# Reading the stationary weight block of the transposed products as every second number of 256

## The chip, the cores and the metric

The kernel runs on one core of one Trainium2 chip. The metric is the device time in microseconds (us) of one execution. Weights lie in HBM in the order in which the host program lays them before the launch; that laying is no part of the time.

## The reference, cut to what matters

Two transformer blocks over 256 tokens of width 2048, in float32. Nearly all of the arithmetic is in eight projections by weight matrices:

```python
z      = rms_norm(x) @ w_in                       # 2048 -> 11264
merged = gate_a * (y_a @ w_branch_a) + gate_b * (y_b @ w_branch_b)
h      = x + merged @ w_out
h      = h + square(relu(rms_norm(h) @ w_up)) @ w_down   # 2048 -> 8192 -> 2048
proj   = rmsnorm(concat(meta, h)) @ w_in_2        # 272 tokens, 2048 -> 6656
h      = h + rmsnorm(concat(ya, yb) @ w_out_2)
```

Between them stand a gated linear recurrence of 8 heads, a banded attention of 16 heads, and in the second block a grouped attention and a differential attention of 8 heads each.

## The kernel before, in words

Every weight matrix is streamed once. It is cut into groups of 512 output columns (`CW`), and a group into 8 chunks of 256 rows (two tiles of 128 rows, 512 columns: 512 KB). A chunk is loaded by SyncE's queue into `raw` (four slots), ScalarE writes its rounded upper part `whi` (L899), VectorE the remainder `wlo = raw - whi` (L1301), both in the type fp32r, and TensorE then makes three products with it: upper by upper, upper by lower, lower by upper. Activations are held in the same two parts (`xhi`/`xlo`, `x2hi`/`x2lo`, `ya_hi`, ...). Semaphores count the chunks: ScalarE waits until TensorE has left the slot, TensorE waits for `wlo_ready`.

There are two ways in which TensorE uses a chunk.

- `chunk_t` (L431 to L448), the transposed one: a block of 128 weight columns is the stationary operand, and the activations (256 tokens, or 272 in the first five groups of `w_in_2`) move past it. The output has the features on the partitions. Per chunk 2 row tiles x 4 blocks x 3 products = 24 matmuls, each of its own weight load. Four blocks of 128 lie side by side in a group, and block b reads columns `slice(b * P, (b + 1) * P)`, 128 adjacent numbers in each partition. All 24 are issued at L446.
- `chunk_n` (L450 to L463), the natural one: 128 tokens of the activations are stationary, and the chunk's 512 columns move. 12 matmuls per chunk, issued at L458.

The transposed way is used for `w_in` except the groups 4, 5, 12 and 13 (18 groups), for `w_branch_a`/`w_branch_b`, `w_up` and all 13 groups of `w_in_2`, the other 8 of which have 256 tokens. The natural one is used for the four other groups of `w_in` and for `w_out`, `w_down` and `w_out_2`.

TensorE runs its instructions in the order of the program: the chunks one after the other, and between them, at places written out by hand, the small matmuls and transposes of the recurrence and of the attentions. `shift_phase` issues three transposes whose output nobody reads. In the recurrence, `level_scores` (L548) has a moving operand whose order depends on the level: 128 numbers of `qp` in runs of 1, 2, 4, ... adjacent numbers (levels 1, 2, 3, ...), while its stationary operand `k_both` is 128 adjacent numbers.

Of the kernel before, what the change touches and what calls it, by code (L numbers as in the profile page):

```python
# [15 lines left out]
P = 128  # L16
# [17 lines left out]
CW = 512  # L34
# [8 lines left out]


C_IN = 0
G_IN = 22
C_BR = C_IN + G_IN * NC
C_OUT = C_BR + 4 * NC
# [13 lines left out]

SETS_BEFORE_2 = (G_IN + 8 + 4 + 32) // 2

# [47 lines left out]
def program(nc, x, w_in, lb_logits, hg_norm_w, rel_bias, w_branch_a, w_branch_b, w_out, norm_mix_w,  # L112
# [3 lines left out]
    with ExitStack() as ctx:  # L116
# [44 lines left out]
        def at(name, kib, shape, dt=F32):  # L161


            with ExitStack() as tmp:
                if kib:
                    tmp.enter_context(nc.sbuf_tensor(name + "_pad", [P, int(kib * 256)], F32))
                return tmp.enter_context(nc.sbuf_tensor(name, shape, dt))
# [21 lines left out]
        pairs = at("pairs", 76, [P, HG, P])  # L189
# [146 lines left out]
        def set_needs():  # L336


            n = [SETS_BEFORE_2 + 3, SETS_BEFORE_2 + 2]
            need = {}  # L340
            for j in range(5, G_IN2):
                s = set_of(j)
                need[j] = n[s]
                n[s] += 1
                if j == 5:
                    n[0] += 1
            return need, n

        need2, sets_before_out2 = set_needs()
        out_free = [G_IN // 2 + 4 + n // 2 + 1 for n in range(4)]  # L350
        down_free = [G_IN // 2 + 8 + 4 * (QUARTERS - 1) + g // 2 + 1 for g in range(4)]

        def wide_hi(kt, n):

            return xw_first[:, kt, 0:n] if kt < WIDE_FIRST else xw_rest[:, kt - WIDE_FIRST, 0:n]
# [10 lines left out]
        def _(sp):  # L366
            def chunk(c0, k, src):

                if not isinstance(c0, int) or c0 + k >= SLOTS:
                    sp.wait_ge(wlo_ready, c0 + k - SLOTS + 1)  # L370
                    sp.sem_inc(sp_turn, 1)
                sp.dma_start(raw[:, k % SLOTS], src).then_inc(raw_in[k % SLOTS], 16)

            def rows(w, k, cols):
                return w[:, CK * k:CK * k + CK, cols]
# [3 lines left out]
            for c in range(4):  # L379
# [6 lines left out]
                else:  # L386
                    chunk(C_IN, c, rows(w_in_t, c, slice(0, CW)))
            for k in range(4, NC):
                chunk(C_IN, k, rows(w_in_t, k, slice(0, CW)))
            with sp.Fori(1, G_IN) as g:  # L390
                for k in range(NC):
                    chunk(C_IN + NC * g, k, rows(w_in_t, k, bass.ds(g * CW, CW)))

# [34 lines left out]
        def _(pe):  # L428
            mm = nc.tensor.matmul

            def chunk_t(c0, k, kt0, xh, xl, outs, n, first, last, shared=True):  # L431

                first_chunk = isinstance(c0, int) and c0 + k == C_IN
                pe.wait_ge(half_lo if first_chunk else wlo_ready, c0 + k + 1)
                for j in range(CK):
                    kt = kt0 + j
                    if first_chunk and j == 1:
                        pe.wait_ge(wlo_ready, 1)  # L440
                    for b in range(4):
                        cols = slice(b * P, (b + 1) * P)
                        x_high = xh[:, kt, 0:n] if xh is not None else wide_hi(kt, n)
                        for i, (w, v) in enumerate(((whi, x_high), (whi, xl[:, kt, 0:n]), (wlo, x_high))):
                            start = first and j == 0 and i == 0 and (b % 2 == 0 or not shared)
                            ins = mm(outs[b], w[:, k % SLOTS, j, cols], v, start=start,  # L446
                                     stop=last and j == CK - 1 and i == 2, skip_group_check=True)
                ins.then_inc(pe_done, 1)  # L448
# [16 lines left out]
            def blocks(s):  # L465
                return [pset(s)[:, b, :] for b in range(4)]
# [14 lines left out]
            def turn_start(c):  # L481

                pe.wait_ge(x_in[c], 16)
                if c >= 2:
                    pe.wait_ge(x_ready, 4 * c - 4)
                for kt in range(4 * c, 4 * c + 4):
                    for t in range(NT):
                        o = (kt % 2) * T + t * P
                        ins = nc.tensor.transpose(ps[:, 4 + (kt % 8) // 2, o:o + P],
                                                  x_nat[:, t, kt * P:(kt + 1) * P], ident[:])  # L490
                    if kt % 2 == 1:
                        ins.then_inc(n_tr, 1)
# [18 lines left out]
            def warm(n):  # L511

                for i in range(n):
                    nc.tensor.transpose(ps[:, 2, 0:P], ident[:], ident[:])
# [100 lines left out]

            for g in range(G_IN):
                c0, s = C_IN + NC * g, g % 2
                if g >= 2:
                    pe.wait_ge(set_free[s], g // 2)
                if g == G_LEVEL:  # L620
                    pe.wait_ge(meta_ready, 1)
                natural = g in (4, 5, 12, 13)
                for k in range(NC):
                    if g == 0:
                        if k == 0:
                            warm(11)
                            turn_start(0)
                            warm(9)
                        if k < 3:
                            turn_start(k + 1)  # L630
                        if k == 3:
                            turn_vectors()
                        if k == 6:
                            row_scale()
                        pe.wait_ge(x_ready, CK * (k + 1))
                    if natural:
                        chunk_n(c0, k, CK * k, uhi, ulo, s, k == 0, k == NC - 1)
                    else:
                        chunk_t(c0, k, CK * k, uhi, ulo, blocks(s), T, k == 0, k == NC - 1)
                    if k == 0 and g == 2:  # L640
                        turn_meta()
                    if k == 1 and G_LEVEL <= g < G_HGOUT:
                        level_scores(g - G_LEVEL)
                    if k == 1 and g == G_HGOUT:
                        hg_output()
                    if k == 7 and g == G_HGOUT:
                        hg_squares()
                    if k == 2 and g == G_HGOUT + 1:
                        pe.wait_ge(hg_sd, 4)
                        shift_phase(4, lambda i: acc[:, i, :])  # L650
                    at = NC * (g - G_ATT) + k
                    for part, late in ((att_values, 5), (att_turn, 4), (att_scores, 0)):
                        if pair_at(at - late) is not None:
                            part(pair_at(at - late))
                    if at == PAIR_STEP * (AH // 2):
                        shift_phase(5, lambda i: prob[:, 0, i * P:(i + 1) * P])
# [1335 lines left out]
    return np.concatenate([np.arange(P), np.arange(T - 1, P - 1, -1)])  # L1992


def shape_constants():

    f32 = np.float32
    identity = np.eye(P, dtype=f32)

    s, t = np.arange(P)[:, None], np.arange(P)[None, :]  # L2000
    masks = np.zeros((P, 8, P), f32)
    masks[:, 0, :] = s == t
    for level in range(1, 8):
        hb = 2 ** (level - 1)
        masks[:, level, :] = (s // (2 * hb) == t // (2 * hb)) & ((s // hb) % 2 != (t // hb) % 2)
    triangles = np.stack([s < t, s > t], axis=1).astype(f32)

    inv_freq = (f32(10000.0) ** (-np.arange(0, DH, 2, dtype=f32) / f32(DH))).astype(f32)
    places = token_order()
    row = np.concatenate([places // 64, np.zeros(META, int)]).astype(f32)  # L2010
    col = np.concatenate([places % 64, np.zeros(META, int)]).astype(f32)
    ang = np.stack([row[:, None] * inv_freq, col[:, None] * inv_freq]).astype(f32)
    half = np.concatenate([ang[0], ang[0], ang[1], ang[1]], axis=1).T
    rope_cos, rope_sin = np.cos(half).astype(f32), np.sin(half).astype(f32)

    turn = np.zeros((P, P), f32)
    for m in range(P):
        if (m // 32) % 2 == 0:
            turn[m + 32, m] = -1.0
        else:  # L2020
            turn[m - 32, m] = 1.0
    qpos = places + META
    kpos = np.concatenate([places + META, np.arange(META)])
    distance = np.abs(qpos[:, None] - kpos[None, :]).astype(f32)
    return {"identity": identity, "level_masks": masks, "rope_cos": rope_cos, "rope_sin": rope_sin,
            "rope_turn": turn, "distance": distance}, {"triangles": triangles}
# [21 lines left out]
```

## Time and profile before

| | us |
|---|---|
| median of 3 runs | 1895.21 |
| lowest and highest run | 1893.33, 1895.46 |
| profiled execution, time | 1893.33 |
| profiled execution, span | 1893.3 |

| engine | busy us | share of the span | instructions |
|---|---|---|---|
| TensorE matmul (PE) | 1879.6 | 99% | 13432 |
| TensorE weight load (PEld) | 1743.7 | 92% | 13432 |
| VectorE (DVE) | 1101.4 | 58% | 1270 |
| ScalarE (ACT) | 889.3 | 47% | 1171 |
| GpSimd (POOL) | 143.6 | 8% | 122 |

How to read it: consecutive matmuls overlap in the records, since each record runs from the start of its operand's reading to a modelled end. The cost of a matmul to the kernel is then the distance from its start to the start of the next one, called its pitch below; durations are only compared with each other. A pitch is read from the start times in a timeline, or from the number of matmuls in a window. A few per cent of the matmul records can be missing, so windows without gaps are used.

### The profile page before, as it was taken

The page shows a single profiled execution, that of the slowest core. Times are in us where ns is not written, and L with a number is a line of the kernel's source. Part 1 is how long each engine was busy: PE and PEld are TensorE (multiplying, and loading weights), DVE is VectorE, ACT ScalarE, POOL GpSimd, SP SyncE. Part 2 cuts the span into 40 slices and gives each one's busy share as a digit, 9 for nine tenths or more (in the row PEclk, how much of TensorE's full clock was granted, in tenths as well). Part 3 has the DMA queues.
Part 4 walks back from the last instruction along what each step waited for, and adds up shares of the span by engine and source line. Part 5 has one row for each costly group of instructions (what it writes and reads, how often), then busy time and mean ns, then how long its engine had stood idle before and what let it go on. Part 6 is the DMA issues. An engine that isn't in the chain of part 4 may idle for free.

```text
span 1893.3 us, 33876 instructions
## 1 busy us (share of the span) xinstructions
PE 1879.6 (99%) x13432; PEld 1743.7 (92%) x13432; DVE 1101.4 (58%) x1270; ACT 889.3 (47%) x1171; POOL 143.6 (8%) x122
## 2 busy tenths in 40 slices
PE   9999999999999999999999999999999999999998
PEld 9989998999999889988998899899889999899986
DVE  6556766667655555545445445445565556767664
ACT  6544444455544445443444344334454355664543
POOL 2001322411001100000010000000010000000000
PEclk9999999999999999999999999999999999999999
DMA  8566565566565656656665665566556655354454
GB/s 270 184 181 177 181 179 178 165 200 180 168 231 191 214 186 179 194 198 192 196 192 193 194 191 194 194 190 190 189 185 181 179 170 150 105 147 144 156 190 143
DMA packets 176434, 346.47 MB, mean 183 GB/s; under 512 B 10976, under 2 KB 11184, under 8 KB 175776
## 3 DMA queue, kind: packets, MB, share of 16 engines
q1 hardware_dynamic: 174176, 337.76, 57.2%
q0 software_dynamic: 2128, 6.82, 1.4%
q8 instruction: 101, 1.65, 0.4%
q14 instruction: 29, 0.24, 0.0%
HBM read 342.44 MB, written 2.10 MB: 182 GB/s over the span
## 4 chain that ended last, share of the span: by engine, by line
PE 97%; DVE 1%; ACT 0%; DMA 0%; issue 0%; SPq 0%; DVEq 0%; ACTq 0%
PE ps L446 58%; PE ps L458 33%; PE ps L548 1%; PE ps L781 1%; DVE wlo L1301 1%; PE ps L771 1%; PE ps L748 1%; PE ps L791 0%; DMA raw<-in_w_in_dram 0%; ACT whi L899 0%; PE ps L476 0%; PE ps L759 0%; PE ps L599 0%; PE ps L591 0%; DVE xlo L1323 0%; PE ps L610 0%
## 5 line engine op out<-in xcount | busy, mean ns | idle before, releaser
L1301 DVE TENSOR_TENSOR wlo<-raw,whi 128x1024 fp32r<-128x1024 f32 x631 | 796.5, 1268 | 698.1 <-ACT whi L899 697.1
L899 ACT ACTIVATE whi<-raw 128x1024 fp32r<-128x1024 f32 x631 | 664.5, 1058 | 886.3 <-PE ps L446 551.5
L446 PE MATMUL ps<-xhi,whi 128*128 128x256 f32 (+1 forms) x1904 | 542.2, 285 | 0.4 <-DVE wlo L1301 0.3
L446 PE MATMUL ps<-xhi,wlo 128*128 128x256 f32 (+1 forms) x1904 | 531.3, 279 | 0.0
L446 PE MATMUL ps<-xlo,whi 128*128 128x256 f32 x1664 | 462.5, 278 | 0.0
L446 PEld LDWEIGHTS ps<-xhi,whi 128*128 128x128 f32 x1904 | 359.1, 189 | 9.3 <-issue 6.7
L446 PEld LDWEIGHTS ps<-xhi,wlo 128*128 128x128 f32 x1904 | 357.8, 188 | 0.0
L446 PEld LDWEIGHTS ps<-xlo,whi 128*128 128x128 f32 x1664 | 313.4, 188 | 1.5 <-issue 0.7
L446 PE MATMUL ps<-x2hi,whi 128*128 128x256 f32 x1024 | 282.8, 276 | 0.0
L446 PE MATMUL ps<-x2hi,wlo 128*128 128x256 f32 x1024 | 282.7, 276 | 0.0
L446 PE MATMUL ps<-x2lo,whi 128*128 128x256 f32 x1024 | 282.7, 276 | 0.0
L446 PEld LDWEIGHTS ps<-x2lo,whi 128*128 128x128 f32 x1024 | 192.2, 188 | 0.2
L446 PEld LDWEIGHTS ps<-x2hi,whi 128*128 128x128 f32 x1024 | 192.2, 188 | 0.2
L446 PEld LDWEIGHTS ps<-x2hi,wlo 128*128 128x128 f32 x1024 | 192.2, 188 | 0.0
L458 PE MATMUL ps<-whi,ya_lo 128*128 128x512 f32 x256 | 100.8, 394 | 0.0
L458 PE MATMUL ps<-whi,yb_lo 128*128 128x512 f32 x256 | 100.8, 394 | 0.0
L458 PE MATMUL ps<-whi,xlo 128*128 128x512 f32 x256 | 100.8, 394 | 0.0
L458 PE MATMUL ps<-wlo,ya_hi 128*128 128x512 f32 x256 | 100.3, 392 | 0.0
L458 PE MATMUL ps<-wlo,yb_hi 128*128 128x512 f32 x256 | 100.2, 392 | 0.0
L458 PE MATMUL ps<-whi,xhi 128*128 128x512 f32 x256 | 100.2, 391 | 0.0
L458 PE MATMUL ps<-wlo,xhi 128*128 128x512 f32 x256 | 100.1, 391 | 0.0
L458 PE MATMUL ps<-whi,ya_hi 128*128 128x512 f32 x256 | 99.7, 390 | 0.0
(373 smaller groups left out, 2370.6 us busy)
## 6 DMA issues: line engine op xcount, KB each, us to landing
raw<-in_w_in_dram SPq DMA_DIRECT2D x279, 512.0 KB, 3.8
raw<-in_w_up_dram SPq DMA_DIRECT2D x128, 512.0 KB, 3.7
raw<-in_w_down_dram SPq DMA_DIRECT2D x128, 512.0 KB, 3.7
raw<-in_w_out_dram SPq DMA_DIRECT2D x64, 512.0 KB, 3.8
raw<-in_w_branch_a_dram SPq DMA_DIRECT2D x16, 512.0 KB, 4.9
raw<-in_w_branch_b_dram SPq DMA_DIRECT2D x16, 512.0 KB, 3.8
x_nat<-in_x_dram SPq DMA_DIRECT2D x4, 512.0 KB, 7.4
rel<-in_rel_turned_dram POOLq DMA_DIRECT2D x8, 256.0 KB, 4.3
```

What stands on the lines that cost most here:

```text
L446: ins = mm(outs[b], w[:, k % SLOTS, j, cols], v, start=start, stop=last and j == CK - 1 and i == 2, skip_group_check=True)
L458: ins = mm(ps[:, 2 * s + t, :], v[:, kt, toks], w[:, k % SLOTS, j, :], start=first and j == 0 and i == 0, stop=last and j == CK - 1 and i ...
L548: ins = mm(misc[:, hd // 4, (hd % 4) * P:(hd % 4 + 1) * P], k_both[:, hd, :], spread(qp[:, hd, 0:1], *both_tiles), start=True, stop=True)
L748: ins = mm(ps[:, 4 + i, 0:TM], qb[f, hd, t * P:(t + 1) * P], kb[f, hd, :], start=True, stop=True)
L771: ins = nc.tensor.transpose(ps[:, 6, i * P:(i + 1) * P], p[:, i * P:(i + 1) * P], ident[:])
L781: ins = mm(ps[:, 7, 0:P], pt2[:, u % 2, i * P:(i + 1) * P], v, start=i == 0, stop=i == 2)
L899: f(whi[:, k % SLOTS], raw[:, k % SLOTS], ACT.Copy).then_inc(whi_ready, 1)
L1301: tt(wlo[:, k % SLOTS], raw[:, k % SLOTS], whi[:, k % SLOTS], ALU.subtract).then_inc(wlo_ready, 1)
```

## The change

`chunk_t` reads block b of a pair as every second number of 256: blocks 0 and 1 are the even and the odd columns of the first 256, blocks 2 and 3 those of the second 256. So that the products stay the same, the host lays the columns of two blocks alternating (`paired`) in `w_branch_a`, `w_branch_b`, `w_up`, `w_in_2`, and in `w_in` except the groups 4, 5, 12 and 13, which are used in the natural way. `chunk_n` is unchanged, as are all loads, waits, tiles and the order of instructions.

```diff
+NATURAL_IN = (4, 5, 12, 13)
...
                     for b in range(4):
-                        cols = slice(b * P, (b + 1) * P)
+                        cols = slice(b // 2 * 2 * P + b % 2, b // 2 * 2 * P + 2 * P, 2)
...
-                natural = g in (4, 5, 12, 13)
+                natural = g in NATURAL_IN
...
+def paired(w, every=True):
+    laid = np.array(w)
+    spans = laid.reshape(*w.shape[:-1], -1, 2, P)
+    pairs = np.swapaxes(spans, -1, -2).reshape(w.shape)
+    if every:
+        return pairs
+    groups = np.arange(w.shape[-1]) // CW
+    return np.where(np.isin(groups, NATURAL_IN), laid, pairs)
...
     laid["x"] = laid["x"][:, places]
+    laid["w_in"] = paired(laid["w_in"], every=False)
+    for name in ("w_branch_a", "w_branch_b", "w_up", "w_in_2"):
+        laid[name] = paired(laid[name])
```

## Rows read from the trace of the kernel before

**Rows 1.** The page: the chain that ended last, by engine and by line

```profile
PE 97%; DVE 1%; ACT 0%; DMA 0%; issue 0%; SPq 0%; DVEq 0%; ACTq 0%
PE ps L446 58%; PE ps L458 33%; PE ps L548 1%; PE ps L781 1%; DVE wlo L1301 1%; PE ps L771 1%; PE ps L748 1%; PE ps L791 0%; DMA raw<-in_w_in_dram 0%; ACT whi L899 0%; PE ps L476 0%; PE ps L759 0%; PE ps L599 0%; PE ps L591 0%; DVE xlo L1323 0%; PE ps L610 0%
```

**Rows 2.** The waits, longest first (us in total, times, longest)

```profile
ACT whi L899 <- PE ps L446: 551.5, 322, 7.0
PE ps L446 <- DVE wlo L1301: 0.3, 1, 0.3
```

**Rows 3.** Windows of L446 alone (stretch: length, PE busy (count), PEld busy (count), clock, DMA)

```profile
30.00:60.00 30.00, 29.80 (x254) 29.70 (x253) 1.00 0.73 229
1080.00:1160.00 80.00, 80.00 (x708) 80.00 (x708) 1.00 0.62 193
```

**Rows 4.** Groups by line and form, TensorE, whole span (count | busy us, mean ns)

```profile
L446 PE MATMUL ps<-xhi,wlo 128*128 128x256 f32 x1664 | 462.5, 278 | 0.0
L446 PE MATMUL ps<-x2hi,wlo 128*128 128x256 f32 x1024 | 282.7, 276 | 0.0
L446 PE MATMUL ps<-xw_lo,whi 128*128 128x272 f32 x320 | 91.7, 287 | 0.0
```

**Rows 5.** Groups by line and form in 30 to 60 us (mean ns behind the comma)

```profile
L446 PE MATMUL ps<-xlo,whi 128*128 128x256 f32 x85 | 23.9, 281 | 0.0
L446 PEld LDWEIGHTS ps<-xlo,whi 128*128 128x128 f32 x84 | 16.1, 192 | 0.0
L446 PEld LDWEIGHTS ps<-xhi,whi 128*128 128x128 f32 x85 | 16.0, 188 | 0.0
```

**Rows 6.** Timeline at 1100 us (start, length, in us)

```profile
1099.99 0.28 PE L446 MATMUL ps<-x2lo,whi 128*128 128x256 f32 x1
1099.99 0.19 PEld L446 LDWEIGHTS ps<-x2hi,wlo 128*128 128x128 f32 x1
1100.10 0.28 PE L446 MATMUL ps<-x2hi,wlo 128*128 128x256 f32 x1
1100.11 0.19 PEld L446 LDWEIGHTS ps<-x2hi,whi 128*128 128x128 f32 x1
1100.22 0.28 PE L446 MATMUL ps<-x2hi,whi 128*128 128x256 f32 x1
```

**Rows 7.** Timeline at 1500 us, TensorE: first and fifth start of 272-column products

```profile
1499.88 0.29 PE L446 MATMUL ps<-xw_lo,whi 128*128 128x272 f32 x1
...
1500.38 0.29 PE L446 MATMUL ps<-xw_rest,wlo 128*128 128x272 f32 x1
```

**Rows 8.** Instructions of L612, L446, L476 (duration ns min/median/max, first and last start us)

```profile
L612 PEld LDWEIGHTS ps<-prob_t,av x32: 137/137/137, 413.2 to 529.3; 128*64 128x64 f32 x32
L446 PEld LDWEIGHTS ps<-x2hi,wlo x1024: 187/188/189, 726.7 to 1339.2; 128*128 128x128 f32 x171
L476 PEld LDWEIGHTS ps<-ident,h x64: 137/141/143, 663.3 to 1436.6; 128*128 128x128 f32 x64
```

**Rows 9.** Instructions of L548 at levels 1, 2 and 3, one window each (same columns)

```profile
L548 PE MATMUL ps<-qp,k_both x16: 324/337/338, 156.6 to 159.1; 128*128 128x128 f32 x16
...
L548 PE MATMUL ps<-qp,k_both x16: 282/283/283, 181.0 to 182.8; 128*128 128x128 f32 x16
...
L548 PE MATMUL ps<-qp,k_both x16: 270/275/275, 204.7 to 206.4; 128*128 128x128 f32 x16
```

**Rows 10.** Windows of L458 alone, in `w_down` (columns as in rows 3)

```profile
840.00:880.00 40.00, 40.00 (x176) 32.84 (x175) 1.00 0.58 190
```

**Rows 11.** Three transposes in the timeline at 1604.7 us, and their mean of one (274 ns)

```profile
1604.74 0.49 PE L771 MATMUL ps<-ident,p 128*128 128x128 f32 x3
...
L771 PE MATMUL ps<-ident,p 128*128 128x128 f32 x96 | 15.9, 274 | 0.8 <-DVE p L1752 0.7
```

**Rows 12.** Groups by line and form in 760 to 800 us

```profile
L1301 DVE TENSOR_TENSOR wlo<-raw,whi 128x1024 fp32r<-128x1024 f32 x15 | 18.3, 1224 | 16.0 <-ACT whi L899 16.0
L899 ACT ACTIVATE whi<-raw 128x1024 fp32r<-128x1024 f32 x15 | 15.7, 1058 | 17.7 <-PE ps L446 17.7
```

## The prediction

> **What bounds the kernel now.** I read the page's chain first: TensorE holds 97% of it, 58% of the span at L446, the matmuls of `chunk_t`, and 33% at L458, the natural ones [rows 1]. Waits do not compete with that: L446 waited 0.3 us for a remainder, while ScalarE stood 551.5 us waiting for L446 to leave a slot [rows 2]. So what a matmul at L446 costs is its pitch, and whatever changes it goes one to one into the span. Their number follows from the code: 18 + 4 + 16 + 8 = 46 groups' worth at 256 tokens (one group of `w_branch_a` and `w_branch_b` together) x 192 = 8832, and 5 x 192 = 960 at 272 tokens.
>
> The pitch has two values. From 1080 to 1160 us 708 records touch 80 us; the first two or so began before it, so 80 / 706 = 113.3 ns. From 30 to 60 us it is 30 / 254 = 118 ns [rows 3]. In the first stretch a matmul takes 276 ns in the records [rows 4]; in the second all take 281, and one weight load in three takes 192 instead of 188 [rows 5]. Work and operands' shapes are the same, so there are two steady rhythms in which the reading of the weights and that of the moving operand get in each other's way by different amounts. The mean of 278 over 1664 of the `xhi`/`xlo` matmuls says that about (278 - 276) / (281 - 276) = 0.4 of their 3 x 1664 are in the slow rhythm, some 1900 (listing the starts gives 1848); the x2 ones are all at 276 [rows 4]. So about 6900 matmuls at 113.3, 1900 at 118. The 272-token ones are at (1500.38 - 1499.88) / 4 = 125 ns, 123.6 over all of them [rows 7].
>
> The clock is granted in full (1.00, the level of 2.4 GHz) throughout [rows 3, 10]. 256 columns at one a cycle are 106.7 ns, so 6.6 ns of 113.3 are something else. A natural matmul has 40 us / 174.5 = 229 ns for 512 columns, that is 213.3 + 16 [rows 10]. The transposes, with a shorter load of 141 ns in place of 188 [rows 8] and a moving time like ours, run at (0.49 - 0.27) / 2 = 0.11, 109 to the nanosecond by their starts [rows 11]: I take 109 as the floor of a pitch of this size.
>
> **The change, part by part.** Nothing but one operand's pattern changes. Number of instructions, DMAs, waits, tiles and the splits by ScalarE and VectorE (which work number by number, whatever column it is) are as before: 0 us. L458 reads adjacent numbers as before: 0 us. Launch and ends lie outside the edit: 0 us.
>
> What is left is the weight load at L446, 9792 times, now 128 numbers 8 bytes apart. No load in this trace is strided, so its cost is bounded by the nearest rows.
>
> How much room has a load? It starts with the matmul before it, within 0.01 us, and its own matmul starts 0.11 us later [rows 6]. A load of 64 columns is recorded at 137 ns, one of 128 at 188 [rows 8]: 51 ns for 64 columns, so 102 ns for 128. Out of a pitch of 113.3 that leaves 11 ns at most, less what a load needs to be started and handed over. Both operands of these matmuls are thus near their limits, about 102 and 107 ns.
>
> What does a stride cost? The nearest row is a moving operand: at level 2 of the recurrence, L548 reads `qp` in runs of two adjacent numbers, at level 3 in runs of four, at level 1 singly. Pitches are (182.8 - 181.0) / 15 = 120 ns, (206.4 - 204.7) / 15 = 113 (112 by the starts) and (159.1 - 156.6) / 15 = 167; durations 283, 275, 337 [rows 9]. These are 128 numbers in about 107 ns, the rate of our load. So runs of four are free, halving them costs 8 ns per 128 numbers, and taking them singly costs 55. Every second number puts two useful numbers where four were: level 2 is the row nearest to it.
>
> I take the 8 ns as the load's added time and ask what of it shows. If the 11 ns were all free it would vanish: lower bound 0 for this mechanism. But the slow rhythm says otherwise: where one load in three takes 4 ns more, all matmuls take 5 more and the pitch rises by 4.4 [rows 5, 3], so a load that meets resistance is paid for by the matmuls. I take the pitch that level 2 itself shows, 120 ns, for both rhythms:
> - 6900 x (120 - 113.3) = 46 us
> - 1900 x (120 - 118) = 4 us
> - 960 at 123.6: already above 120, the longer matmul covers the load: 0 us.
>
> Sum 50 us. Upper bound of the same mechanism: 8 ns on top of each rhythm and of the 272 ones, 9792 x 8 = 78 us; if a pair were to count as single numbers, 55 x 9792 = 540 us, which I hold for 2 in 100 and leave out of the range. Below nothing: the pitch could fall to the floor of 109, see the second rival.
>
> Against the profiled execution: 1893.3 + 50 = 1943; it was the fastest of three, 1.9 below their median, so 1945 is forecast. As TensorE is all of the path, nothing else becomes late: ScalarE and VectorE only idle longer.
>
> The Trainium skill speaks against this price. Its page "SBUF — State Buffer", section "Door 1: The DMA port swizzle", says that memory lines are 16 bytes and that two hits per line are enough to absorb the access time; two 4-byte numbers of four in a line are just that, and the sum by it would be 0. Level 2 has two hits per 16 bytes too and lost 8 ns, so here the trace disagrees, for a moving operand. By that rule the result is the first rival.
>
> **The rivals.**
> 1. *The load's stride is absorbed.* For it: the load has up to 11 ns of room, more than 8; a load may be read ahead differently from a moving operand. Against it: the coupling in the slow rhythm. Time: 1895, or with another share of slow rhythm a few us beside it (all fast: -1900 x 4.4 = -8 us, 1887; all slow: +6900 x 4.4 = +30 us, 1925; the last I count with the slower case).
> 2. *The collisions end: faster.* One mechanism: now the moving operand goes through four numbers while the load goes through two, so the two walk through the memory at different speeds and meet again and again, which is the 6.6 ns (and, met badly, 11). With a stride of two the load covers as many bytes per time as the moving operand, the two keep their distance, and the pitch falls to 109. It decides from where the distance stays constant, that is, if load and moving operand take the same time. For it: two rhythms exist at all, so the relative place matters; the excess is there in every fp32r matmul, while transposes with a short load are at 109. Against it: the natural matmuls lose 16 ns of 229 although no load is under way in the second half of each, so most of the excess seems to belong to the moving operand alone. Price: 6900 x 4.3 + 1900 x 9 + 960 x 7 = 30 + 17 + 7 = 54 us: 1841; half of it 1868.
>
> The page "TensorE: Matmul & The Clock Gate", Part 2, says the load has a read port of its own and takes no bandwidth from the running matmul. By it neither the forecast's coupling nor rival 2 would exist; the 192-ns loads beside 281-ns matmuls [rows 5] disagree.
>
> 3. *Both slow down*: double the collisions, 124 ns and more: 6900 x 10.7 + 1900 x 6 + 960 x 4 = 89 us: 1984.
>
> Should the pitch fall, the feeding holds: a chunk is 24 matmuls, 2.62 us at 109, against 1.22 for VectorE's and 1.06 for ScalarE's part [rows 12].
>
> **How the numbers follow.** Slower by the load (forecast, 1920 to 1975) 0.42, both slow down 0.08, absorbed 0.15 (of which a part falls outside plus or minus 0.2% because the share of rhythms moves), collisions end 0.35. A measurement of this kernel can tell about 0.2%, 3.8 us, from no change. Slower: 0.42 + 0.08 + 0.02 = 0.52; within 0.2%: 0.09; faster: 0.35 + 0.04 = 0.39. The forecast's own range is 1920 to 1975. The range to hold 8 in 10 must reach into the faster case: 1848 to 1975.
>
> **What would show it.** Right: in 1080 to 1160 us (shifted) the L446 pitch near 120, matmul durations about 283, loads 192 to 197; L458 still 229 and 388 to 394. Absorbed: 113.3 and 276. Collisions end: about 109 to 111, durations 270 to 272, and no stretch at 118. A pitch at 118 everywhere with loads of 192 would be the slow rhythm, the forecast's mechanism at its smaller size. I am wrong in mechanism if L446 falls, and if the 272-token matmuls move while the 256-token ones do not.

## The result

The change made the kernel slower: 1947.18 us median (1946.49 to 1947.5, 4 runs) against 1894.27 (1892.75 to 1895.46, 4 runs), ratio 1.0276, 95% interval 1.0261 to 1.029. The forecast was 1945.

### The profile after

The page's busy line and the chain, shares by line; `chunk_t`'s matmuls are L447 here, `chunk_n`'s L459 (compare [rows 1]):

```profile
PE 1932.4 (99%) x13432; PEld 1796.9 (92%) x13432; DVE 1099.4 (57%) x1270; ACT 890.0 (46%) x1171; POOL 143.5 (7%) x122
...
PE ps L447 60%; PE ps L459 32%; PE ps L549 1%; PE ps L782 1%; PE ps L749 1%; PE ps L772 1%; DVE wlo L1302 0%; PE ps L792 0%; DMA raw<-in_w_in_dram 0%; PE ps L477 0%; PE ps L760 0%; ACT whi L900 0%; PE ps L600 0%; PE ps L592 0%; DVE xlo L1324 0%; PE ps L611 0%
```

TensorE is busy 52.8 us longer with the same number of instructions, and the span grew by 52.2 (1893.3 to 1945.5). The other engines' busy time is the same within 2 us. ScalarE waits longer for L447 than it did in [rows 2]:

```profile
ACT whi L900 <- PE ps L447: 611.9, 332, 7.2
ACT whi L900 <- PE ps L459: 318.9, 200, 5.3
```

Windows of L447 alone, one in the first groups of `w_in`, one in `w_up` (columns as in [rows 3]):

```profile
30.00:60.00 30.00, 29.80 (x249) 29.62 (x248) 1.00 0.72 220
1310.00:1350.00 40.00, 40.00 (x336) 40.00 (x335) 1.00 0.58 181
```

The second gives 40 / 334 = 119.8 ns, 120.0 by the starts; the first 120 too. The two rhythms of before, 113.3 and 118, are one now. Groups by form, and the loads (to compare with [rows 4, 8]):

```profile
L447 PE MATMUL ps<-x2hi,wlo 128*128 128x256 f32 x1024 | 289.5, 283 | 0.0
...
L447 PE MATMUL ps<-x2lo,whi 128*128 128x256 f32 x1024 | 288.0, 281 | 0.0
```

```profile
L447 PEld LDWEIGHTS ps<-x2hi,whi x1024: 193/193/199, 748.6 to 1381.6; 128*128 128x128 f32 x171
L447 PEld LDWEIGHTS ps<-x2lo,whi x1024: 193/195/199, 748.9 to 1381.8; 128*128 128x128 f32 x171
```

Matmuls are recorded at a mean of 281 to 283 ns instead of 276, loads at 193 to 195 instead of 188. The natural matmuls kept 229 ns by their starts. Those of 272 tokens went from 123.6 to 126.8; in the timeline at 1550 us it is 0.89 us for seven:

```profile
1549.76 0.29 PE L447 MATMUL ps<-xhi,whi 128*128 128x272 f32 x1
...
1550.65 0.29 PE L447 MATMUL ps<-xw_lo,whi 128*128 128x272 f32 x1
```

The sum closes with the measured 52.9 us: 6900 x 6.7 + 1900 x 2.3 + 960 x 3.2 = 46 + 4 + 3 = 53 us.

### The profile page after: what moved, and what is told of

It is laid out like the page before. It is cut to its first block, busy times and chain, and to the rows that moved or that the text cites. A ratio compares the mean times of both kernels' runs of the same rounds, so it can differ in the third digit from the quotient of the medians.

```text
span 1945.5 us, 33876 instructions
## 1 busy us (share of the span) xinstructions
PE 1932.4 (99%) x13432; PEld 1796.9 (92%) x13432; DVE 1099.4 (57%) x1270; ACT 890.0 (46%) x1171; POOL 143.5 (7%) x122
## 3 DMA queue, kind: packets, MB, share of 16 engines
q8 instruction: 102, 1.67, 0.3%
## 4 chain that ended last, share of the span: by engine, by line
PE 97%; DVE 1%; DMA 0%; ACT 0%; issue 0%; SPq 0%; DVEq 0%; ACTq 0%
PE ps L447 60%; PE ps L459 32%; PE ps L549 1%; PE ps L782 1%; PE ps L749 1%; PE ps L772 1%; DVE wlo L1302 0%; PE ps L792 0%; DMA raw<-in_w_in_dram 0%; PE ps L477 0%; PE ps L760 0%; ACT whi L900 0%; PE ps L600 0%; PE ps L592 0%; DVE xlo L1324 0%; PE ps L611 0%
## 5 line engine op out<-in xcount | busy, mean ns | idle before, releaser
L447 PE MATMUL ps<-xhi,whi 128*128 128x256 f32 (+1 forms) x1904 | 549.7, 289 | 0.3 <-DVE wlo L1302 0.3
L447 PE MATMUL ps<-xhi,wlo 128*128 128x256 f32 (+1 forms) x1904 | 537.8, 282 | 0.0
L447 PE MATMUL ps<-xlo,whi 128*128 128x256 f32 x1664 | 469.4, 282 | 0.0
L447 PEld LDWEIGHTS ps<-xhi,whi 128*128 128x128 f32 x1904 | 369.6, 194 | 9.2 <-issue 7.0
L447 PEld LDWEIGHTS ps<-xhi,wlo 128*128 128x128 f32 x1904 | 369.7, 194 | 0.0
L447 PEld LDWEIGHTS ps<-xlo,whi 128*128 128x128 f32 x1664 | 323.1, 194 | 1.3 <-issue 0.7
L447 PE MATMUL ps<-x2hi,wlo 128*128 128x256 f32 x1024 | 289.5, 283 | 0.0
L447 PE MATMUL ps<-x2hi,whi 128*128 128x256 f32 x1024 | 288.4, 282 | 0.0
L447 PE MATMUL ps<-x2lo,whi 128*128 128x256 f32 x1024 | 288.0, 281 | 0.0
L447 PEld LDWEIGHTS ps<-x2lo,whi 128*128 128x128 f32 x1024 | 199.2, 195 | 0.2
L447 PEld LDWEIGHTS ps<-x2hi,whi 128*128 128x128 f32 x1024 | 198.6, 194 | 0.2
L447 PEld LDWEIGHTS ps<-x2hi,wlo 128*128 128x128 f32 x1024 | 198.2, 194 | 0.0
L459 PE MATMUL ps<-whi,xlo 128*128 128x512 f32 x256 | 100.6, 393 | 0.0
L459 PE MATMUL ps<-whi,xhi 128*128 128x512 f32 x256 | 100.6, 393 | 0.0
L459 PE MATMUL ps<-whi,ya_lo 128*128 128x512 f32 x256 | 100.6, 393 | 0.0
L459 PE MATMUL ps<-whi,yb_lo 128*128 128x512 f32 x256 | 100.5, 393 | 0.0
L459 PE MATMUL ps<-whi,ya_hi 128*128 128x512 f32 x256 | 100.5, 393 | 0.0
L459 PE MATMUL ps<-whi,yb_hi 128*128 128x512 f32 x256 | 100.3, 392 | 0.0
L459 PE MATMUL ps<-wlo,xhi 128*128 128x512 f32 x256 | 99.9, 390 | 0.0
L459 PE MATMUL ps<-wlo,ya_hi 128*128 128x512 f32 x256 | 99.8, 390 | 0.0
```

What stands on the lines that cost most here:

```text
L459: ins = mm(ps[:, 2 * s + t, :], v[:, kt, toks], w[:, k % SLOTS, j, :], start=first and j == 0 and i == 0, stop=last and j == CK - 1 and i ...
```

## The experiments

All kernels are the one before with the edit shown, unless it says otherwise. What had to be told apart: is it the load that needs longer (A), do its additional reads delay the moving operand (B), does the size of the stride count or the fact of one, and why do both rhythms become one.

### The stride where the load has room

```diff
-                        toks = slice(t * P, (t + 1) * P)
+                        toks = slice(t, T, 2)        # chunk_n
```

> The kernel before, with the stride put where the load has room: in the natural products (L458, 2688 of them, 512 columns moving, pitch 229 ns) the stationary tokens are read as every second of 256; L446 stays adjacent. The order of tokens inside a group of 256 comes out changed, so values differ from the reference's. Theory A (the strided load itself takes 6 to 8 ns longer, and this shows only where the pitch is set by the load): loads at L458 go from 188 to about 194, matmuls and pitch stay at 229, time as before within 0.2%, 1892 to 1898. Theory B (the strided load reads twice as many lines, and each of these reads delays the moving operand): the same 6.7 ns per load are paid here too, pitch about 236, 2688 x 6.7 = 18 us, time about 1912.

Measured: 1921.12 us, ratio 1.0141 (1.0124 to 1.0158). That is neither of the two numbers. The loads of L458, two of its matmul groups, and a window in `w_down`:

```profile
L458 PEld LDWEIGHTS ps<-whi,ya_hi x256: 194/194/198, 820.2 to 1440.5; 128*128 128x128 f32 x128
```

```profile
L458 PE MATMUL ps<-wlo,ya_hi x256: 392/394/398, 820.5 to 1441.0; 128*128 128x512 f32 x128
...
L458 PE MATMUL ps<-whi,yb_hi x256: 392/396/398, 831.5 to 1452.0; 128*128 128x512 f32 x128
```

```profile
850.00:890.00 40.00, 40.00 (x173) 33.45 (x172) 1.00 0.55 191
```

40 / 171.5 = 233.3 ns by the starts too, against 229: although the load has more than 100 ns to spare there, the moving operand lost 4.4 ns, 2688 x 4.4 = 12 us. So theory B is real, at two thirds of its supposed size, and theory A alone falls. The other 14 us are in matmuls that nobody touched. This window lies in `w_up`:

```profile
760.00:800.00 40.00, 40.00 (x342) 1.00 0.64 192
```

40 / 340 = 117.7 ns, where it had been 113.3: L446 entered `w_up` in the slow rhythm and stayed in it in all 16 groups, 3072 x 4.4 = 13.5 us. The rhythm is thus not a property of the place: the same instructions with the same loads run in one or the other. It is not settled by the program alone either. The stretch from 30 to 60 us, at 118 ns in [rows 3], is at 113 in this run, although no changed instruction runs before 102.6 us:

```profile
30.00:60.00 30.00, 29.80 (x263) 29.62 (x262) 1.00 0.73 229
```

What decides at the start of a stretch, chance or the chip used perhaps, is not shown.

### The stride's size

```diff
-                        cols = slice(b * P, (b + 1) * P)
+                        cols = slice(b, CW, 4)          # every fourth, host layout to match
```

```diff
+                        cols = slice(b, b + 3 * P, 3)   # every third, no new layout
```

> The change with a stride of four instead of two: block b of a group is every fourth column of the 512, laid so by the host. Theory A in its form by lines (what counts is how many of the four numbers of 16 bytes are used): one number per line, as level 1 of the recurrence at L548, which took 55 ns more than adjacent numbers; the load grows from 188 to some 240, pitch of L446 about 165, time 1894 + 9792 x 50 = about 2380. Theory S (a stride other than one costs a fixed amount, whatever its size): pitch 120 as with a stride of two, time about 1947.

> The kernel before with every third number as stationary block at L446, no new layout (the columns taken are not the right ones, so the values differ). 128 numbers then touch 96 lines of 16 bytes instead of 64 (stride two), 32 (adjacent) or 128 (stride four). Theory A by lines: a cost between that of two (6.7 ns) and of four, about 25 to 35 ns: time 2140 to 2240. Theory S: 120 ns and 1947.

Measured: 3051.72 us (ratio 1.6104) with every fourth, 2489.05 us (ratio 1.3135) with every third. The loads, and a window in `w_up`, of stride four:

```profile
L447 PEld LDWEIGHTS ps<-x2hi,whi x1024: 308/330/331, 1232.0 to 2212.3; 128*128 128x128 f32 x171
```

```profile
1500.00:1540.00 40.00, 40.00 (x174) 1.00 0.39 109
```

The same two of stride three:

```profile
L446 PEld LDWEIGHTS ps<-x2hi,whi x1024: 252/263/268, 987.2 to 1793.9; 128*128 128x128 f32 x171
```

```profile
1300.00:1340.00 40.00, 40.00 (x228) 1.00 0.41 128
```

Pitches by the starts: 233.2 and 176.6 ns. Both runs missed both of their numbers. A fixed price per stride is refuted, and so is the price taken from level 1 of L548 (55 ns; measured 120). What fits is a count: 128 numbers at stride 4, 3, 2 touch 128, 96, 64 different groups of four numbers, and 233.2 / 128 = 1.82, 176.6 / 96 = 1.84. At stride 2 that makes 64 x 1.83 = 117 ns.

Three limits of this count. At strides up to four it grows just as the length of memory that a load spans, so these runs cannot tell the two apart. That a group has four numbers is not in these runs either; it comes from level 3 of the recurrence, whose runs of four take 112 ns [rows 9]: groups of eight, at twice the price, would need 32 x 3.66 = 117. And the adjacent load touches only 32 groups, 58 ns by the count; it is limited by something else, as the next runs show.

### What the load needs alone

Each matmul of `w_up` cut into two of 128 columns with a load each, once with adjacent numbers, once in the changed kernel:

```diff
-                            ins = mm(outs[b], w[:, k % SLOTS, j, cols], v, start=start,
...
+                            for c in range(0, n, m or n):
+                                ins = mm(outs[b][:, c:c + (m or n)], w[:, k % SLOTS, j, cols], v[:, c:c + (m or n)],
+                                         start=start and c == 0,
...
-                        chunk_t(c0 + NC * g, k, CK * k, x2hi, x2lo, blocks(g % 2), T, k == 0, k == NC - 1)
+                        chunk_t(c0 + NC * g, k, CK * k, x2hi, x2lo, blocks(g % 2), T, k == 0, k == NC - 1, m=P)
```

> The kernel before, with every matmul of w_up (3072 of L446's) cut into two of 128 columns, each with its own weight load of 128 adjacent numbers. The moving operand now needs 53 ns, so the pitch is what the load needs alone. Line theory (one 16-byte line per about 1.8 ns and stream at most, 1.2 numbers per ns otherwise): 32 lines do not bind, 128 numbers take 102 to 107 ns, pitch 107 to 111, w_up's part grows by 3072 x (2 x 109 - 113.3) = 322 us, time about 2215. If the load were no limit near 107, the pitch would be well below 100 and the time below 2150.

> The changed kernel (stride of two everywhere at L446) with the same cut of w_up's matmuls. Line theory: the load needs 64 x 1.82 = 117 ns whatever the moving operand does, pitch about 117 to 120 in w_up; time 1947 + 3072 x (2 x 118 - 120) = about 2303, loads 188 + 8 or more. Collision theory (the load is slower only because a moving operand at full speed reads at the same time; here that operand stands still half of the time): pitch as in the run with adjacent numbers, 107 to 112, time about 2260.

Measured: 2233.66 and 2303.43 us, near the 2215 and at the 2303 of the line theory, away from 2150 and 2260. A window in `w_up`, adjacent first, then strided:

```profile
760.00:800.00 40.00, 40.00 (x361) 1.00 0.32 93
```

```profile
770.00:810.00 40.00, 40.00 (x342) 1.00 0.34 95
```

40 / 359 = 111.4 and 40 / 340 = 117.6 ns (111.6 and 117.8 by the starts). With half as many columns to move per load the stride still costs 6.2 of its 6.7 ns: it is the load that needs longer. And the 117.8 ns are the 64 groups at 1.84, in line with strides three and four. One thing could spoil the reading of 111.6 ns as the need of the adjacent load: a matmul of 128 columns is recorded as long here as one of 256 (275 and 276 ns), so its record does not show that its columns take only half the time.

```profile
L447 PE MATMUL ps<-x2hi,whi 128*128 128x128 f32 x91 | 17.6, 275 | 0.0
```

The trace of before speaks for the load, by matmuls in plain float32. Eight of 512 columns behind one another (L577) start 429 ns apart, 107 per 128 columns; 128 columns with an adjacent load of 128 for each (L542) start 111.5 ns apart, more than the columns need.

```profile
368.25 3.59 PE L577 MATMUL ps<-o_hg,ones 128*128 128x512 f32 x8
...
L542 PE MATMUL ps<-qp,kr x32: 271/275/275, 131.1 to 134.5; 128*128 128x128 f32 x32
```

So before the change the pitch of 113.3 was within 2 ns of what the load alone needs; the 11 ns of room that I had computed from recorded durations did not exist. In the changed kernel the pitch of 120.0 is 2.2 ns above the 117.8 of the load alone; no run shows where these 2.2 ns go.

### The stride on the moving operand

```diff
-ins = mm(ps[:, 2 * s + t, :], v[:, kt, toks], w[:, k % SLOTS, j, :],
+ins = mm(ps[:, 2 * s + t, :], v[:, kt, toks], spread(w[:, k % SLOTS, j, 0:1], [1, 2], [2, CW // 2]),
```

> The kernel before, with the stride of two on the other operand: at L458 the 512 weight columns move as the 256 even, then the 256 odd ones (columns of the output change places, so values differ), loads adjacent. Line theory: 256 + 256 half-used lines are 256 lines at least 1.8 ns each, 461 ns, pitch 229 -> about 460, 2688 x 232 = 624 us, time about 2518. If the reading were limited by numbers and not by lines: pitch 229 to 245, time 1895 to 1940.

Measured: 2501.75 us, ratio 1.3202, close to the line theory's 2518; a window in `w_down`:

```profile
1000.00:1040.00 40.00, 40.00 (x90) 1.00 0.30 105
```

40 / 88.5 = 452, by the starts 453.5 ns for 256 groups of four, 1.77 ns each. With adjacent numbers it is 229 / 128 = 1.79. One figure fits both operands from a stride of two on: at most one group of four float32 numbers per about 1.8 ns. It would also account for the 16 ns of 229 in [rows 10], which I had left unexplained, since the 213.3 ns reckoned in the prediction for 128 groups are 1.67 per group; no run tests this against a fixed price per matmul. The Trainium skill ("SBUF — State Buffer", section "Door 1: The DMA port swizzle") names lines of 16 bytes, which agrees with groups of four; its rule that two hits in a line absorb the access does not hold here, for the load (6.2 ns) or for the moving operand (453.5 against 229 ns).

### Not all loads strided

The fences show the columns of the stationary operand alone; for half of the blocks the host lays out the columns to match.

```diff
+   cols if w is whi else slice(b // 2 * 2 * P + b % 2, b // 2 * 2 * P + 2 * P, 2)    # one load in three
```

```diff
+                        cols = slice(b, 2 * P, 2) if b < 2 else slice(b * P, (b + 1) * P)    # half of the blocks
```

```diff
+   slice(0, 2 * P, 2) if b % 2 == 0 and i == 2 else cols    # one in six; b == 0: one in twelve
```

> The kernel before, with the stride of two only in the loads of the remainder wlo, one load in three at L446 (the remainder is then taken from other columns than the upper part, so the values differ). If every strided load costs its own 6.7 ns (A), a third of the 53 us of the change: time about 1894 + 18 = 1912, pitches 113, 113, 120 in turn. If one strided load is enough to put all matmuls into a slower rhythm (as one load of 192 ns in three goes with 118 ns for all before): pitch 118 to 120 for all, time 1930 to 1947.

> The change for blocks 0 and 1 of each group alone; blocks 2 and 3 lie and are read as before. Six loads with stride and six without follow each other. If each load pays for itself: half of the 53 us, 1894 + 26 = 1920, pitches near 120 and 113. If the rhythm, once slow, holds on until something other than the loads breaks it (as one load in three cost as much as three): 1935 to 1947.

> The kernel before, with one strided load in twelve at L446: only the remainder's load of block 0 (it takes other columns than it should, a small part of the values). One load in three had cost 20 ns per strided load, all loads 6.7 each. If the 20 ns belong to a lone strided load with its successors: 816 x 20 = 16 us, time 1911. If a lone one costs its own 6.7 ns and the third's price came from never getting back to the fast rhythm: 816 x 6.7 = 5.5 us, time 1900, and eight or more of the twelve pitches at 113.

> The same with one strided load in six (the remainder's, of blocks 0 and 2). At 20 ns per strided load: 1632 x 20 = 33 us, time 1928. At 6.7 ns: 11 us, 1906. If the rhythm cannot come back within six matmuls: all at 120, 1945.

Measured: one in three 1944.92 us (ratio 1.0263, 1.0246 to 1.028), half of the blocks 1927.3 (1.0171, 1.0154 to 1.0188), one in twelve 1904.13 (1.0051, 1.0038 to 1.0065), one in six 1918.41 (1.0127, 1.0111 to 1.0142). One load in three cost nearly as much as all three, and each of the other three runs came out between its expected numbers. The loads of one in three, of which only the third kind is strided, and a matmul beside an adjacent load:

```profile
L446 PEld LDWEIGHTS ps<-x2hi,whi x1024: 187/188/190, 748.0 to 1380.9; 128*128 128x128 f32 x171
L446 PEld LDWEIGHTS ps<-x2lo,whi x1024: 188/189/192, 748.2 to 1381.0; 128*128 128x128 f32 x171
L446 PEld LDWEIGHTS ps<-x2hi,wlo x1024: 194/195/198, 748.3 to 1381.1; 128*128 128x128 f32 x171
```

```profile
L446 PE MATMUL ps<-x2lo,whi x1024: 280/283/283, 748.3 to 1381.1; 128*128 128x256 f32 x171
```

The timeline with one in twelve shows why; the load of the matmul at 1301.07 is the strided one:

```profile
1300.84 0.28 PE L446 MATMUL ps<-x2hi,whi 128*128 128x256 f32 x1
1300.95 0.28 PE L446 MATMUL ps<-x2lo,whi 128*128 128x256 f32 x1
1301.07 0.28 PE L446 MATMUL ps<-x2hi,wlo 128*128 128x256 f32 x1
1301.19 0.28 PE L446 MATMUL ps<-x2hi,whi 128*128 128x256 f32 x1
1301.31 0.28 PE L446 MATMUL ps<-x2lo,whi 128*128 128x256 f32 x1
1301.43 0.28 PE L446 MATMUL ps<-x2hi,wlo 128*128 128x256 f32 x1
1301.54 0.28 PE L446 MATMUL ps<-x2hi,whi 128*128 128x256 f32 x1
```

To the nanosecond the pitches are 113, 115, 120, 122, 115, 115, 113: a lone strided load costs 20 ns. Its own matmul starts only 2 ns late; the rest is in the four pitches after it, beside adjacent loads. One in three makes 113.3 + 20 / 3 = 120.0, and with three in three the mean is the same 120.0: five pitches are lengthened by one strided load, so the next comes before the last is paid off. With one in six the sum is 1632 x 20 = 33 us, less the slow rhythm that it ends (1848 x 4.4 = 8 us): 25; measured 24.6. With one in twelve it is 16 less up to 8; measured 10.3. With half of the blocks, twelve pitches in `w_up` sum to 1413 ns instead of 1360: 816 x 53 = 43, less 8 again, 35; measured 32.2. My price of 6.7 ns for a lone one was wrong, and that of 20 held for less than its whole, as the second effect was not in the expectation. Why matmuls behind an adjacent load go on paying is not settled: a guess is that the reading of the two operands is out of its fast order and needs some matmuls to come back to it, but nothing here shows the reads themselves.

### Strided loads against the slow rhythm

From 480 to 490 us every pitch of L446 was 117 to 119 ns before. With one strided load in twelve the mean there is 115.5, and most pitches between the strided loads are 113 or 114: the slow rhythm has ended. (The stretch at 40 us, on which the next expectation rests, went back too, but the first experiment had it at 113 with no strided load in it.) The last kernel uses this: adjacent loads, but in 18 chunks, with which slow stretches begin, six strided loads each. The calls that pass `alternate` and the host's laying are left out of the fence. One group of three transposes is left out of this kernel as well.

```diff
+ALT_IN = (3, 6, 7, 8 * 15, *(8 * 16 + 5 * i + 1 for i in range(1, 8)))
+ALT_IN2 = tuple(8 * 5 + i for i in (0, 2, 26, 46, 50, 55, 59))
...
                         cols = slice(b * P, (b + 1) * P)
+                        if alternate and j == 0 and b < 2:
+                            cols = slice(b, 2 * P, 2)
...
-                    if k == 2 and g == G_HGOUT + 1:
-                        pe.wait_ge(hg_sd, 4)
-                        shift_phase(4, lambda i: acc[:, i, :])
```

> The kernel before, adjacent loads everywhere, except that in 18 chunks (of 408 transposed ones) the first row tile's blocks 0 and 1 are laid alternating and read with a stride of two, 6 strided loads each; the chunks are those with which stretches of the slow rhythm (118 ns) begin, and one shift_phase is left out. In the run with one strided load in twelve the stretch at 40 us went back to 113 after each of them. If a few strided loads break the slow rhythm: some 57 chunks x 24 x 4.4 ns = 6.0 us gained, 18 x 47 ns = 0.85 us paid, 0.3 us saved with the transposes: about 5.5 us faster, 1888.5. If the slow rhythm depends on what is computed or read there and not on how it was entered: 0.5 us slower, 1894.5, and 118 again in those stretches.

Measured: 1889.51 us (1888.83 to 1890.68, 11 runs) against 1894.3 (15 runs), ratio 0.9975, 95% interval 0.9966 to 0.9984. All engines in 480 to 490 us, before and in this kernel (PE's count is what to compare; by the starts the pitch of the transposed products there went from 117.8 to 113.5):

```profile
480.00:490.00 10.00, 10.00 (x86) 9.84 (x87) 6.09 (x13) 5.70 (x14) 1.41 (x2) 1.00 0.65 176
```

```profile
480.00:490.00 10.00, 10.00 (x91) 10.00 (x90) 6.34 (x12) 7.53 (x16) 1.89 (x4) 1.00 0.57 170
```

By the starts, 8150 of the 8832 matmuls run below 116 ns (6838 before) and 499 between 116 and 120 (1848 before): 1350 x 4.4 = 5.9 us gained, 0.9 us paid. The 11 runs of this kernel all lie below the 15 of the one before, so the gain is real, a quarter of a per cent. Not all of it need be due to the strided loads: some 250 matmuls of the gain, 1.1 us, lie between 30 and 60 us, a stretch that was at 113 ns without them in the first experiment and in the cut `w_up` with adjacent numbers, before anything changed there had run; and what leaving out the three transposes does by itself was not run.

## Why the prediction was right

- *TensorE's pitch at L446 goes one to one into the span*: right, 52.8 us more busy, 52.2 us longer span.
- *Price of the load, 8 ns by level 2 of the recurrence*: right in kind, near in size. Alone the load lost 6.2 ns (111.6 to 117.8). The row was nearest because it too takes half of each group of four; 64 groups at about 1.8 ns are 117. That the difference of two levels was nearly the difference for the load is in part luck: the 112 ns of level 3, from which I counted the 8, are the need of its own adjacent load (L542: 111.5), not the time of the moving operand (107).
- *Pitch 120 for both rhythms*: right, and to the digit by luck. The step that led to it, that the load's delay is passed on, was argued from the slow rhythm; the runs with cut matmuls show a simpler cause, that the load was within 2 ns of the limit and now needs 117.8. Those 117.8 ns explain 4.5 of the 6.7 ns; the other 2.2 are measured but not explained. My 11 ns of room came from 51 ns of recorded duration per 64 columns, and was at most 2.
- *272-token matmuls: 0 us*: wrong by 3 us. A load of 117.8 ns fits into their 123.6, yet they went to 126.8: they lost 3.2 ns beside a load that had room, as the natural ones lost 4.4 in the first experiment.
- *Rival 1, absorbed*: out. With more than 100 ns of room the stride still cost 4.4 ns per matmul.
- *Rival 2, collisions end*: the pitch rose to 120 where it should have fallen to 109. That the same work has two rhythms, from which it argued, is so, and gave the last kernel.
- *Rival 3, both slow down, 124 ns*: the loads do slow the moving operand (4.4 ns in the natural products), but at L447 the pitch rose by 6.7 ns, not by 10.7 or by the 6.2 and 4.4 together.
- *540 us if pairs count as single numbers*: they don't, but single numbers cost more than level 1 had said: 120 ns, not 55. I had read level 1 as one number per group. Its order is 0, 129, 2, 131, 4, ... (`[2 * hb, P // (2 * hb)], [P + hb, 2], [1, hb]` with `hb` = 1): it touches 64 different groups, each twice, with another group in between. By the count that is 117 ns if the second touch is free and 233 if it costs as much as the first; it took 167 [rows 9], between the two. The count does not hold for such an order, and no run shows what does.

## What to carry to other kernels

Where an operand is read with a stride, count the groups of four float32 numbers that it touches, and do it for the stationary operand as well: here each group cost about 1.8 ns on either side, at strides of two to four for the load and of two for the moving operand. A load of 128 adjacent numbers already needed 111.6 ns, nearly as long as the 256 columns that were to hide it. A price for a strided operand is best read from a strided row of the same trace, with the order in which it goes through memory. Where the same matmul shows two pitches in different stretches, look at where each stretch begins and ends: the pitch holds on until something disturbs it. And look at a second run before explaining one stretch, since the same instructions can come out at 118 ns in one and at 113 in another.

## What was not expected of the hardware

- A single strided load of 128 numbers lengthened five pitches in a row (20 ns in all), and its own matmul started only 2 ns late.
- The steady pitches of L446 are few: in threes they sum to 340, 353 and 360 ns (113.3, 117.7, 120.0), and one strided load in three gives the same 360 as three in three.
- With an edit in one stage the pitch of an untouched one was 4.4 ns longer, 3072 times, because it ran in the slow rhythm; and a few strided loads, each by itself a loss, with three transposes left out, made the kernel 0.25% faster.
